# A one-core attention and recurrence block: stores of split weights, raw tiles for the weight sums, and tile 2's residual and output stores change their places

## The reference, cut to what matters

```python
h = rmsnorm(x, w_norm_pre[l])
proj = h @ w_in[l]                       # 1024 -> 3328 columns
q_a, k_a, v_a, z_a, q_r, f_r, i_r, z_r = jnp.split(proj, SPLIT_POINTS, axis=-1)
o_a = sliding_window_sink_attention(rope(q_a), rope(k_a), v_a, attn_sinks[l]) * jax.nn.silu(z_a)
o_r = rmsnorm(hgrn2_chunkwise(q_r, f_r, i_r, lb), hgrn_norm[l]) * jax.nn.silu(z_r)
y = jnp.concatenate([o_a, o_r], axis=-1) @ w_out[l]
x = x + rmsnorm(y, w_norm_post[l])       # the residual: x is read again here
```

## Time and profile before

| what | value |
| --- | --- |
| median of 3 runs | 883.18 us |
| the profiled execution's own time | 880.8 us |
| its span | 879.0 us |
| TensorE busy | 855.7 us (97%) |
| VectorE, ScalarE, GpSimd busy | 635.3, 520.4, 114.6 us |
| read from DRAM, written | 157.95 MB, 52.43 MB |
| chain that ended last | PE 64%, DVE 16%, ACT 8%, DMA 6% |

### The profile page before, as it was taken

The page is one execution under the profiler, slowest core; times in us unless marked ns, Lnnn a source line. Parts: engine busy times, 40 slices in busy tenths (PEclk is TensorE's granted clock), DMA queues, the critical chain, the costliest instruction groups (busy, mean ns, idle before and its releaser), DMA issues.

```text
span 879.0 us, 12449 instructions
## 1 busy us (share of the span) xinstructions
PE 855.7 (97%) x4430; PEld 701.4 (80%) x4430; DVE 635.3 (72%) x1125; ACT 520.4 (59%) x1033; POOL 114.6 (13%) x84
## 2 busy tenths in 40 slices
PE   7999999999998999999999999999998999999997
PEld 6887888888786778888888878887886887888785
DVE  6878868763665899767346789887775367988846
ACT  7766456673574558567246555865842755676544
POOL 0000013520200000433020000144300000004210
PEclk9999999999999999999999999999999999999999
DMA  8685755649967954453779684454799574444496
GB/s 317 233 312 197 282 201 178 230 144 389 413 220 268 399 223 163 172 198 114 260 282 339 221 358 174 147 178 173 254 381 369 193 286 144 144 144 164 165 324 258
DMA packets 59981, 211.20 MB, mean 240 GB/s; under 512 B 6672, under 2 KB 6928, under 8 KB 59920
## 3 DMA queue, kind: packets, MB, share of 16 engines
q1 hardware_dynamic: 57184, 203.46, 63.2%
q10 hardware_dynamic: 2736, 6.95, 2.0%
HBM read 157.95 MB, written 52.43 MB: 239 GB/s over the span
## 4 chain that ended last, share of the span: by engine, by line
PE 64%; DVE 16%; ACT 8%; DMA 6%; issue 4%; SPq 1%; POOL 0%; DVEq 0%; ACTq 0%
PE bank L569 44%; DMA kept_lo<-w_lo 3%; PE bank L825 2%; PE bank L578 2%; PE turn_b L825 2%; PE score_b L825 2%; DVE kv_tok L1356 2%; DMA w_lo<-kept_lo 2%; PE score_b L602 2%; PE turn_b L626 1%; PE turn_b L578 1%; PE score_b L578 1%; DVE q_gate L1449 1%; PE turn_b L679 1%; PE bank L670 1%
## 5 line engine op out<-in xcount | busy, mean ns | idle before, releaser
L569 PE MATMUL bank<-h_hi,w_hi 128*128 128x512 f32 x832 | 325.4, 392 | 8.7 <-DMA w_lo<-kept_lo 7.7
L569 PE MATMUL bank<-h_hi,w_lo 128*128 128x512 f32 x832 | 327.4, 394 | 0.0
L569 PE MATMUL bank<-h_lo,w_hi 128*128 128x512 f32 x832 | 326.2, 392 | 0.0
L569 PEld LDWEIGHTS bank<-h_hi,w_hi 128*128 128x128 f32 x832 | 156.6, 188 | 42.4 <-DMA w_lo<-kept_lo 9.0
L569 PEld LDWEIGHTS bank<-h_lo,w_hi 128*128 128x128 f32 x832 | 156.4, 188 | 34.8 <-issue 3.3
L569 PEld LDWEIGHTS bank<-h_hi,w_lo 128*128 128x128 f32 x832 | 156.4, 188 | 32.9 <-issue 0.2
L1681 POOL TENSOR_TENSOR mix_lo<-v_r,mix_hi 128x512 fp32r<-128x512 f32 x16 | 21.1, 1322 | 550.0 <-ACT v_r L1113 550.0
L1234 DVE TENSOR_TENSOR w_lo<-w_raw,w_hi 128x1024 fp32r<-128x1024 f32 x37 | 45.9, 1248 | 33.6 <-ACT w_hi L899 33.1
L1356 DVE STREAM_TRANSPOSE kv_tok<-k_mid 32x128 f32<-32x128 f32 x192 | 58.1, 302 | 2.8
L899 ACT ACTIVATE w_hi<-w_raw 128x1024 fp32r<-128x1024 f32 x38 | 39.8, 1051 | 22.9 <-issue 10.3
L914 ACT ACTIVATE g_a<-g_a 128x512 f32<-128x512 f32 x32 | 20.3, 633 | 40.3 <-DVE g_a L1314 40.3
(11 more groups left out here) (265 smaller groups left out, 1551.4 us busy)
## 6 DMA issues: line engine op xcount, KB each, us to landing
w_hi<-kept_hi SPq DMA_DIRECT2D x108, 512.0 KB, 3.8
w_lo<-kept_lo SPq DMA_DIRECT2D x108, 512.0 KB, 4.7
w_raw<-in_weights SPq DMA_DIRECT2D x46, 512.0 KB, 5.8
kept_hi<-w_hi SPq DMA_DIRECT2D x34, 512.0 KB, 6.3
kept_lo<-w_lo SPq DMA_DIRECT2D x34, 512.0 KB, 7.2
x_in<-in_x_rows SPq DMA_DIRECT2D x8, 1024.0 KB, 7.7
x_in<-in_x SPq DMA_DIRECT2D x15, 512.0 KB, 7.3
out<-q_gate ACTq DMA_DIRECT2D x9, 512.0 KB, 8.4
```

What stands on the lines that cost most here:

```text
L569: mm = pe.matmul(acc(w)[:, :], stationary[:, s, k, :], moving[:, k, :], start=(m == 0), stop=(m == 3 * KT - 1), skip_group_check=True)
```

## The change

The change moves instructions and adds none to the arithmetic.

1. `SUMS_IN`, `SUMS_AT` and `SUMS_OUT` go from 6, 5 and 12 to 8, 6 and 13: in tiles 1 and 2 the four raw tiles are loaded behind the pair of weight 8 and not of weight 6, the four parts of the sums run in steps 6 to 9 and not 5 to 8, and the results are stored behind the pair of weight 13.
2. The last three saves of split weights (running numbers 37, 38 and 39) are issued together ahead of tile 1's pair for weight 7. Before, one stood behind each of the pairs for weights 6, 7 and 8.
3. Tile 2's residual is loaded behind the pair for weight 1 of tile 3, and not ahead of the pair for weight 0. Tile 2's output is stored by SyncE, behind the pair for weight 3 of tile 3, and not by ScalarE.
4. In the tile that uses the fast scheme and has a next one (tile 2), VectorE makes `x_low` ahead of the finished rows.

```diff
-SUMS_IN, SUMS_OUT = 6, 12
-SUMS_AT = 5
-RES_AT = ((WT - 3, WT - 1),) * FAST + ((P3B, P3B),) * (TILES - FAST - 1) + ((H0, H0 + 1),)
+SUMS_IN, SUMS_OUT = 8, 13
+SUMS_AT = 6
+RES_AT = ((WT - 3, WT - 1),) * FAST + ((None, None),) * (TILES - FAST - 1) + ((H0, H0 + 1),)
...
+            def store_y(t, stores):
+
+                for b, cols, pieces in stores:
+                    sp.wait_ge(finished.sem, finished.after(t, pieces - 1))
+                    sp.dma_start(out[bass.ds(t * N + b * P, P), cols[0] * N:(cols[-1] + 1) * N].rearrange("p (h n) -> p h n", n=N),
+                                 q_gate[:, 2 * b + cols[0]:2 * b + cols[-1] + 1, :]).then_inc(stored[b // 2], 16)
...
-                    if LATE + RAW_SLOTS <= i < FRESH + RAW_SLOTS:
+                    if LATE + RAW_SLOTS <= i <= FRESH:
                         save_split(i - RAW_SLOTS)
+                    if i == FRESH + 1:
+                        for late in range(FRESH + 1 - RAW_SLOTS, FRESH):
+                            save_split(late)
...
+                    if w == 1 and t > FAST:
+                        load_residual(t - 1, 0)
+                        load_residual(t - 1, 1)
+                    if w == RAW_SLOTS - 1 and t > FAST:
+                        store_y(t - 1, STORES)
...
-                    for b, cols, pieces, pool_pieces in STORES if t >= FAST else PLAIN_STORES:
+                    for b, cols, pieces, pool_pieces in PLAIN_STORES if t < FAST else ():
...
-                for i in range(2) if t + 1 < TILES else ():
-                    post_last(t, i)
+                if t + 1 < TILES:
+                    for i in range(2):
+                        post_last(t, i)
+                    dve.wait_ge(x_high, t + 1)
+                    dve.tensor_tensor(mix_lo[:, 0, :], x_acc[:, :], mix_hi[:, 0, :], ALU.subtract).then_inc(x_low, 1)
                 dve.wait_ge(res_loaded, t * 32 + 32)
...
-                if t + 1 < TILES:
-                    dve.wait_ge(x_high, t + 1)
-                    dve.tensor_tensor(mix_lo[:, 0, :], x_acc[:, :], mix_hi[:, 0, :], ALU.subtract).then_inc(x_low, 1)
```

More of the change, by code:

```diff
@@ L105 @@
 V_PLACE = tuple(range(V_TILE + 1, V_TILE + 5))
-STORES = ((2, (0, 1), 2, 0), (3, (0,), 3, 0), (3, (1,), 4, 0), (0, (0, 1), 6, 0), (1, (0, 1), 8, 0))
-LAST_STORES = STORES[:-1] + ((1, (0,), 7, 0), (1, (1,), 8, 0))
+STORES = ((2, (0, 1), 2), (3, (0,), 3), (3, (1,), 4), (0, (0, 1), 6), (1, (0, 1), 8))
+LAST_STORES = STORES[:-1] + ((1, (0,), 7), (1, (1,), 8))
 PLAIN_STORES = ((0, (0, 1), 1, 1), (1, (0, 1), 3, 0), (2, (0, 1), 4, 2), (3, (0,), 5, 0), (3, (1,), 6, 0))
-SUMS_IN, SUMS_OUT = 6, 12
-SUMS_AT = 5
-RES_AT = ((WT - 3, WT - 1),) * FAST + ((P3B, P3B),) * (TILES - FAST - 1) + ((H0, H0 + 1),)
+SUMS_IN, SUMS_OUT = 8, 13
+SUMS_AT = 6
+RES_AT = ((WT - 3, WT - 1),) * FAST + ((None, None),) * (TILES - FAST - 1) + ((H0, H0 + 1),)
 def forget(h):
@@ L531, in _ @@
                         load_residual(t, 1)
[L532 to L538, removed]
+            store_y(TILES - 1, LAST_STORES)
             sp.wait_ge(stored[0], 32 * TILES + 48)
```

## The result

The changed kernel takes 887.87 us, the median of 7 runs (886.4 to 890.11), and the kernel before, timed beside it, 883.18 us (880.53 to 885.0, 7 runs). The ratio is 1.0051, with a 95% interval of 1.0037 to 1.0065: **slower by 0.5%, 4.7 us**. Forecast were 890.8 us, +7.6. The profiled executions differ by more than the medians: span 886.1 against 879.0, +7.1 us.

A forecast was written before the change was run, and what follows sets the result against it. TensorE, busy in 97% of the span, was taken as the bound, so only its gaps could give. +4.3 (tile 1) + 5.9 (tile 2) - 3.35 (tile 3) + 0.8 (clock) = +7.6 on 883.2: 890.8 us, range 883.5 to 896.5.

The forecast's parts named there:

- The waits for weights go: TensorE's waits for weight pairs vanish, costing 6.0 us in tile 1 (lower clock included) and 3.35 us in tile 3.
- Tile 1, +4.3 forecast: Raw tiles land at 270.2 behind 8.4 MB queued, so L626 comes at 300.9, against 296.64: +4.3 us.
- The landing of the raw tiles: Tile 1: saves at 307 GB/s, the rest at 406 GB/s, 2.5 us fixed; raw tiles land at 270.2.
- Tile 2, +5.9 forecast: Raw tiles land at 485.6, one more part of the sums follows weight 6's gate; L626 comes at 516.3: +5.9 us.
- The chain from the gate of weight 6 to L634: Tile 2: VectorE and ScalarE in turn, 24.14 us plus 2.27 us for one more part of the sums, 26.41 us.
- Tile 3, -3.35 forecast: With the residual no longer ahead, weight 0's pair lands at 656.8 and TensorE's wait goes: -3.35 us.
- the next thing late is the residual: Tile 3: tile 2's residual leaves at 655.3 and lands at 664.5; the finals end at 669.9.
- The rival that put weight 4's pair late: Tile 3: weight 4's pair lands past 682.5, up to 3.35 us return as a new wait: 894.2 us; chance 0.12.
- The clock, +0.8 forecast: TensorE's new waits in tiles 1 and 2 lower its clock: 0 to 3.2 us, taken as 0.8.
- Raw tiles in time: Rival at VectorE's step 6: raw tiles land in time, -3.4 us in all, 879.8 us; chance 0.10.
- cancelling: Rival: tile 1 comes out at zero, tile 2 at +3.1, tile 3 at -3.35: 883.0 us; chance 0.08.
- That the second waits each cost 1.6 us more by their clock: Rival in tiles 1 and 2: every wait costs its clock, sum 2.4 us higher, 893.2 us; chance 0.15.

The follow-up runs named there:

- Experiment 4: Changed kernel with sums' numbers back at 6, 12, 5; saves 37 and 38 ahead of weight 6's pair, 39 ahead of weight 7's: 873.59 us, 0.9885.
- experiment 1: Kernel before with only parts 3 and 4 of the change (tile 2's residual, stores and x_low): 877.9 us, ratio 0.9934.
- Experiment 3: Changed kernel with SUMS_IN alone back at 6, the four parts of the sums still at steps 6 to 9: 879.64 us, ratio 0.9967.
- Experiment 8: Experiment 4 with tile 2's five stores issued by ScalarE, as in the kernel before: 872.32 us, ratio 0.9878.
- the two repeats: The kernel before, unchanged, profiled a second and a third time: 883.0 and 883.31 us.
- before_b: The kernel before, unchanged, profiled a second time: 883.0 us.
- experiment 6: Changed kernel with SUMS_IN alone at 7, so the raw tiles leave one weight earlier: 882.48 us, ratio 0.9993.
- experiment 2: Changed kernel with only part 1 undone (SUMS_IN, SUMS_OUT, SUMS_AT back at 6, 12, 5), saves kept together: 875.78 us, ratio 0.9908.
- experiment 5: Changed kernel with SUMS_AT alone back at 5, raw tiles late as in the change: 893.46 us, ratio 1.0125.
- experiment 7: Experiment 4 with x_low behind the finished rows again, as in the kernel before: 874.97 us, ratio 0.9918.

## Why the prediction was right, and where a size was off

The forecast was slower, with 890.8 us and a range of 883.5 to 896.5; measured were 887.87. Step by step:

**The waits for weights go.** Right. None is left in the list, in tile 1 or tile 3. Experiment 4 shows the tile 1 half of it without the raw tiles (-5.6 us), experiment 1 the tile 3 half alone (-3.7 us). Forecast were 6.0 and 3.35.

**Tile 1, +4.3 forecast, +3.1 measured.** The landing of the raw tiles was estimated from queued bytes at 270.2, and part 0 began at 269.89; the gate of weight 6 stood at 274.21 (274.5), L634 at 300.51 (300.9). The absolute times are right within 0.4 us. What makes the term 1.2 too large is 0.7 us that this execution lost ahead of tile 1, most of it in its first 10 us and none of it the change's, and the 0.4. Counted from the pair of weight 6, which left at 245.16 and not at 244.50, the raw tiles were there after 24.7 us where the sum had 25.7; so it is luck that the absolute times agree so well. That the two rates erred in opposite directions is luck too: 277 GB/s were moved from 244 to 256 us, and then 415, where I had 307 and 406.

**Tile 2, +5.9 forecast, +7.0 measured.** The chain from the gate of weight 6 to L634 was forecast as 26.41 us and is 26.30, in both tiles. Off is the landing: 490.66 is 11.4 us behind weight 8's pair, and the sum had 10.2. The mis-sized term is the time that 3.15 MB need behind an idle queue. The stretch moved 337 GB/s over 11.4 us, which is 3.8 MB and not 3.15: the 0.7 MB more are of the pair of weight 9, issued at 484.66 and the only thing that stood behind the raw tiles until 490.10, so its bytes moved before the last raw tile had landed. I had counted the bytes ahead and none behind, and at 406 GB/s 0.7 MB are 1.6 us (an estimate). The 1.2 us of the landing less 0.1 of the chain are the 1.1. With 11.4 us and +7.0 this lies a little beyond the latest that the prediction allowed in tile 2 (11.1 us, +6.8). Experiment 3 (+2.1) and the 4.9 us that remain show both parts of the term.

**Tile 3, -3.35 forecast, -3.6 measured.** Right, and the next thing late is the residual, as named: 664.5 plus the 10.8 us by which tile 2 ended later is 675.3, and the finished rows began at 676.23. It costs nothing. The rival that put weight 4's pair late fell: the pair left at 682.08 (671 + 10.8 = 681.8 forecast), 10.6 us ahead of need.

The Trainium skill (DMA: Bandwidth & Descriptors, "Queues, rings and completion order") has it that the DMA engines alternate between the rings of SyncE and ScalarE. Experiment 8 puts the stores back onto ScalarE's ring, and tile 3 nets -3.7 us in both. So the order has no effect on the time here; with 10.6 us of cover for weight 4's pair, this doesn't say whether the transfers themselves took turns.

**The clock, +0.8 forecast.** Wrong in both directions. In the changed kernel it costs nothing that can be seen in tiles 1 and 2: the granted clock fell to 0.69 and 0.62 behind the turning waits, but L634 still waited for VectorE's chain, so the slow matmuls lay in time that was lost anyway. The prediction gave this reason for the first wait of each pair and still kept a price for the second; the second waits were 1.20 and 0.68 us, where it had about 4, and the clock behind the one of tile 1 was 1.00. And the clock that the *kernel before* loses was taken from a single execution. Its weight waits stand where nothing else is late, so each can cost up to 2.9 us of slow matmuls on top, or none; the profiled execution had none at tile 3, and two others had. That is how the profile's +7.1 becomes +4.7 in the medians: against the spans of the two repeats, 881.2 and 881.5, the changed kernel's 886.1 is 4.9 and 4.6 more. The changed kernel's profiled execution took 887.87 us, its median exactly; that of before took 880.8, 2.4 below its own. I saw the 2.4 and put the difference of one execution on top of it as a constant; as far as the repeats show, it was the price of the very waits that the change removes. Shown are the waits, the clocks and the sizes in three executions of before, and that its timed runs are slow where their mean clock is low. In which place a timed run lost its clock is not shown, since it leaves no trace; that no other difference has a part in the 2.4 us is argued.

**The rivals.** Raw tiles in time and cancelling fell by the same row (part 0 at 269.89 in tile 1). That the second waits each cost 1.6 us more by their clock had little to act on: they were 1.20 and 0.68 us, and the clock behind the one of tile 1 was 1.00. The Trainium skill (TensorE: Matmul & The Clock Gate, "HAM oscillation — how this bites in real kernels") says that transfer waits of some 3 to 5 us between bursts of matmuls send the array to its slow clock each time; the trace of before_b agrees at 3.09 us (0.50), that of the first profile disagrees at 3.35 us (1.00).

**The better version.** The change carries a gain of some 8 us (883.65 to 875.78) and pays some 12 for it. The gain is in the saves and the residual; the loss is all in `SUMS_IN`, `SUMS_AT` and `SUMS_OUT`. Leaving these at 6, 5 and 12 gives 875.78 us, and splitting the saves around weight 6's pair 873.59 (ratio 0.9885, 0.9866 to 0.9904); with the stores issued by ScalarE it is 872.32, which can't be told from it.

## What to carry to other kernels

When a load and its consumer are both moved, compare them with each other, not with their old places: here the load moved by two weights and the consumer by one, and the engine between them took the wait to TensorE. Bytes queued behind one another predicted the landings here to about 1 us, and the same queue's landing moved by 1.7 us between two executions (experiments 4 and 8); where the consumer's engine has no slack (0.18 us at L626), that landing is the time of the kernel. And before an estimate from one profiled execution is put onto a median, ask which waits in it could have cost more in the others: take a second and third profile of the kernel before, and look at where its mean granted clock lies among those of the timed runs.

## What the runs showed of the hardware that I had not expected

- Waits of 2.35 to 3.35 us of TensorE at one and the same place were followed by a granted clock of 1.00 in one execution and of 0.50 to 0.77 in another (3.35: 1.00, 3.09: 0.50, 2.66: 0.77 at tile 3's weight 0; 2.35: 1.00 and 0.66 at tile 2's L634 in experiments 3 and 6; 2.90: 1.00 and 2.83: 0.54 at tile 1's weight 7 in experiments 2 and 3). Ahead of tile 1's weight 8, waits of 3.25 to 3.29 us were followed by 0.50 to 0.55 in all three profiles of the kernel before.
- A slow clock costs only where TensorE is what is late behind it: 0.62 for 7.9 us in tile 2 was followed by 0.68 us of waiting for ScalarE, so nothing was lost by it; 0.66 for 5 us behind L634 cost about 1.6 (3.7 against 2.1).
- Weight 1 of the first tile begins 0.5 to 4.6 us later than in the first profile of before, whatever the kernel (0.9 and 1.4 in its repeats; 4.6 in experiment 6). Where it is 2.5 us or more, the granted clock was down there (0.51 in experiment 6 and 0.76 in 2, 5 and 7, from 10 to 17 us; 1.00 in the others). Two profiles should be compared from tile 1 on.
- A transfer that is issued later can move bytes before an earlier one in the same queue has landed: 3.8 MB went from the pair of weight 8 to the landing of tile 2's raw tiles in the changed kernel, 0.7 MB more than these two hold.
